# Moving the rank-one products, the query decay and the pooling sums of a retention-and-experts step between engines

## The reference, cut to what matters

```python
def step(S, xs):                      # prompt: two chunks of 128 rows, 4 heads
    qc, kc, vc = xs
    scores = jnp.einsum('bhid,bhjd->bhij', qc, kc) * mask
    intra = jnp.einsum('bhij,bhjv->bhiv', scores, vc)
    cross = jnp.einsum('bhid,bhdv->bhiv', qc * q_dec[..., None], S)
    S_new = S * c_dec[:, None, None] + jnp.einsum('bhjd,bhjv->bhdv', kc * k_dec[..., None], vc)
    return S_new, intra + cross
```

```python
outs.append((hi - lo) / cnt[None, :, None])
pooled = jnp.concatenate(outs, axis=-1) - p.astype(jnp.float32)
```

## Time and profile before

| what | us |
|---|---|
| median of 3 runs | 1198.78 |
| the three runs | 1196.62, 1198.78, 1198.88 |
| the profiled execution's own time | 1199.12 |
| its span, first to last instruction | 1197.3 |
| the mixer, routing included, about | 0 to 280 |
| experts, about | 280 to 1197 |

### The profile page before, as it was taken

One profiled execution on the slowest core, in us unless ns is written; L12 is line 12 of the kernel. 1 busy time (PEld: TensorE's weight loads), 2 busy tenths in 40 slices (PEclk: granted clock), 3 DMA queues, 4 the chain that ended last, 5 costly groups with the idle time before them and its releaser, 6 DMA issues.

```text
span 1197.3 us, 15344 instructions
## 1 busy us (share of the span) xinstructions
PE 1141.8 (95%) x5979; PEld 587.2 (49%) x5979; DVE 387.9 (32%) x881; ACT 188.1 (16%) x432; POOL 40.9 (3%) x69
## 2 busy tenths in 40 slices
PE   9989989999999999999989999989998989999997
PEld 7988979985433334333434333434333333333342
DVE  5667755762222122222212121213121212121222
ACT  2132423012011101111010101010101101010112
POOL 3106000000000000000000000000000000000000
PEclk9999989999999999999999999999999999999999
DMA  9753668897999999999999999999999999999996
GB/s 321 226 200 107 226 206 316 291 347 302 426 416 428 426 431 426 429 430 431 423 434 426 434 427 434 423 431 427 436 425 435 421 430 429 436 424 430 427 420 251
DMA packets 66810, 455.22 MB, mean 380 GB/s; under 512 B 4321, under 2 KB 39597, under 8 KB 45760
## 3 DMA queue, kind: packets, MB, share of 16 engines
q1 hardware_dynamic: 64544, 447.99, 90.9%
q0 software_dynamic: 1872, 5.95, 1.5%
q10 hardware_dynamic: 344, 0.61, 0.1%
HBM read 448.65 MB, written 6.11 MB: 380 GB/s over the span
## 4 chain that ended last, share of the span: by engine, by line
PE 62%; DMA 32%; DVE 2%; ACT 1%; SPq 1%; issue 1%; DVEq 0%; ACTq 0%
PE psum L1376 23%; DMA ring<-in_w_down 20%; PE psum L1387 11%; PE psum L1121 11%; DMA ring<-in_w_gate_up 11%; PE psum L1463 4%; PE psum L1286 3%; PE psum L1443 1%; PE psum L1497 1%; PE psum L1148 1%; PE psum L1453 1%; SPq L700 1%; PE psum L1498 1%; DMA ring<-in_w_in 1%; DMA ring<-v_rows 1%
## 5 line engine op out<-in xcount | busy, mean ns | idle before, releaser
L1376 PE MATMUL psum<-ring,x_T 128*64 128x512 f32 x1004 | 454.3, 598 | 9.6 <-DMA ring<-in_w_gate_up 8.9
L1377 PE MATMUL psum<-ring,x_T 128*64 128x512 f32 x994 | 449.3, 599 | 0.0
L1376 PEld LDWEIGHTS psum<-ring,x_T 128*64 128x64 f32 x1004 | 130.5, 137 | 274.2 <-issue 251.8
L1387 PE MATMUL psum<-ring,act_T 128*64 128x512 f32 x960 | 219.1, 610 | 23.2 <-DMA ring<-in_w_down 23.2
L1387 PEld LDWEIGHTS psum<-ring,act_T 128*64 128x64 f32 x960 | 71.1, 140 | 159.3 <-issue 141.7
L1377 PEld LDWEIGHTS psum<-ring,x_T 128*64 128x64 f32 x994 | 129.1, 137 | 0.0
L2517 DVE TENSOR_TENSOR h_raw<-psum,params 128x512 f32<-128x512 f32 x32 | 22.1, 691 | 299.7 <-PE psum L1443 299.7
L2534 DVE TENSOR_TENSOR z_T<-z_T,psum 128x264 f32<-128x264 f32 x112 | 43.0, 426 | 204.5 <-PE psum L1498 204.5
L1121 PE MATMUL psum<-x_sums,ring 128*128 128x132 f32 (+1 forms) x512 | 68.1, 283 | 7.0 <-ACT qk L1727 5.0
L1463 PE MATMUL psum<-normed,one_hot 128*128 128x512 f32 x168 | 74.4, 592 | 0.0
L1121 PEld LDWEIGHTS psum<-x_sums,ring 128*128 128x128 f32 x512 | 63.8, 195 | 7.9 <-ACT qk L1727 5.4
(11 more groups left out here) (347 smaller groups left out, 1002.9 us busy)
## 6 DMA issues: line engine op xcount, KB each, us to landing
ring<-in_w_gate_up SPq DMA_DIRECT2D x32, 4096.0 KB, 31.7
ring<-in_w_gate_up SPq DMA_DIRECT2D x59, 2048.0 KB, 29.7
ring<-in_w_down SPq DMA_DIRECT2D x56, 2048.0 KB, 33.5
ring<-in_w_in SPq DMA_DIRECT2D x21, 1024.0 KB, 6.3
ring<-in_w_down SPq DMA_DIRECT2D x12, 1024.0 KB, 27.3
spare<-in_w_gate_up SPq DMA_DIRECT2D x5, 1280.0 KB, 36.7
ring<-in_state_ret POOLq DMA_DIRECT2D x8, 512.0 KB, 7.7
ring<-v_rows SPq DMA_DIRECT2D x8, 512.0 KB, 8.9
```

What stands on the lines that cost most here:

```text
L1376: mm(psum[0:CAP, 2 * j + n], x, gate, start=first, stop=final)
L1377: last = mm(psum[CAP:P, 2 * j + n], x, up, start=first, stop=final)
L1387: last = mm(psum[j * CAP:(j + 1) * CAP, 4 + n], hidden[:, j, 4 * h + i], w, start=h == 0 and i == 0, stop=h == 1 and i == 3)
```

## The change

Four things move, and no arithmetic is left out.

1. GpSimd issues the loads of states 4 to 7 once the last value tile is done (`tile_done`), ahead of the store of the value rows; before, they stood behind it. The spread of rows 0 to 3 moves from behind the chunk of group 4 to behind the chunk of group 5 (`SPREAD_AT` 8 to 9).
2. Rank-one products 0 to 3 stay on ScalarE but move into groups 4 and 5 (one each) and group 6 (two). Products 4 to 7 go to GpSimd, as one 128x1024 operation each.
3. The decayed queries are made by GpSimd, two operations of 128x512; TensorE's products o and one `more_sums` of VectorE wait for them by `pool_step`.
4. GpSimd's pooling sums begin only when VectorE has written the norm of o (1).

```diff
-RANK_ONE_AT = {1: (0,), 2: (1,), 3: (2,), 4: (3, 4), 5: (5,), 6: (6, 7)}
-SPREAD_AT = 8
+SPREAD_AT = 9
...
+            pool.wait_ge(u_ready, KD)
+            pool.wait_ge(tile_done, done_count(V0 + 7))
+            for b in range(4, NS):
+                pool.dma_start(state_s(b), state_ret[0, b].rearrange("h d v -> d h v")).then_inc(state_in[b], 16)
             pool.wait_ge(aux_took, AUX_AT[("v", 7)] + 1)
             for h in range(H):
                 pool.dma_start(v_rows[:, h], v_few[32 * h:32 * h + NS]).then_inc(v_saved, 16)
-            pool.wait_ge(u_ready, KD)
-            for b in range(4, NS):
-                pool.dma_start(state_s(b), state_ret[0, b].rearrange("h d v -> d h v")).then_inc(state_in[b], 16)
+
+            def rank_one(b):
+
+                pool.wait_ge(spread_in[b % 4], 16 * (b // 4 + 1))
+                nc.gpsimd.tensor_tensor(spread_v[:, b % 4], spread_v[:, b % 4],
+                                        k_cols[:, :, b:b + 1].broadcast_to([P, H, DV]),
+                                        ALU.mult).then_inc(rank_one_ready, 1)
...
             step(nc.gpsimd.tensor_copy(k_cols, k_T[:, :, NPR:NT]))
+            pool.wait_ge(roped, 8)
+            pool.wait_ge(product_done, PRODUCT_AT[3, 3])
+            for c in range(2):
+                step(nc.gpsimd.tensor_tensor(qd[:, c], q_T[:, :, c * P:(c + 1) * P],
+                                             const("q_dec").rearrange("p (h i) -> p h i", h=H), ALU.mult))
 
             n = NM + NPR
+            pool.wait_ge(aux_took, AUX_AT[("o", 1)] + 1)
             for g, w in enumerate(WINDOWS):
...
             nc.gpsimd.memset(both_squares, 0.0).then_inc(zeroed, 1)
+            pool.wait_ge(rank_one_ready, 4)
+            for b in range(4, NS):
+                rank_one(b)
...
+                    pe.wait_ge(pool_step, 2 + c)
...
+                    if g >= GATE_FROM - 2:
+                        rank_one(g - GATE_FROM + 2)
...
+                    if g == GATE_FROM:
+                        rank_one(2)
...
                     if g == GATE_FROM:
+                        rank_one(3)
                         root(0)
...
-                    for b in RANK_ONE_AT.get(g - GATE_FROM, ()):
-                        rank_one(b)
...
-                    V.tensor_tensor(qd[:, c], q_T[:, :, c * P:(c + 1) * P],
-                                    const("q_dec").rearrange("p (h i) -> p h i", h=H), ALU.mult)
...
                 elif g == GATE_FROM + 1:
                     dve.wait_ge(aux_took, AUX_AT[("score", 1)] + 1)
+                    dve.wait_ge(pool_step, 3)
```

## The result

The changed kernel takes 1185.51 us (median of 4 runs, 1184.83 to 1186.14) and the kernel before, in the same runs, 1198.83 (1196.62 to 1200.83). The ratio is 0.9889, interval 0.9871 to 0.9907: faster by 13.3 us. The profiled execution of after took 1186.14 us, its span is 1184.3 (before 1199.12 and 1197.3), the mean granted clock 0.992 (before 0.988).

What follows compares the result with a forecast made beforehand. It took TensorE's mixer stops for ScalarE's copies, with the half clock behind them, as the cost to remove: 1199.1 less 10.0 (stops), less 4.5 (clock), plus 0.9 (chunk of group 6), plus 1.7 (competition) gives 1187.2 us, range 1183 to 1190.

Steps and rivals of the forecast that it cites:

- The stops, 10.0: TensorE's waits in the mixer for ScalarE's copies (5.0, 3.0 and 2.0 us) all go, saving 10.0 us.
- the clock, 4.5: Half-speed clock after TensorE's two long mixer stops goes with them, saving 1.65 + 2.9 = 4.5 us.
- Part 1: Earlier state loads: group 4's chunk lands at 60.0, not 63.8; 3.0 us stop goes; queue sharing delays group 3's 2.3 us.
- The chunk of group 6, +0.9: Spread rows ahead of group 6's chunk delay it; TensorE waits longer at the meta state, +0.9 us (0 to 2).
- Part 2: Rank-one products: ScalarE's fit idle time, GpSimd's take 2.6 us each; 5.0 + 2.0 us of TensorE stops go.
- Part 3 and 4: Query decay on GpSimd is worth nothing; later pooling sums move their competition with VectorE into groups 7 to 10.
- Competition, +1.7: GpSimd's work lengthens VectorE's operations in groups 7 to 13, costing 1.7 us, bounds 0 and 9.6.
- rival D: Gain hidden by the experts' weight stream if not tied to the mixer: 1193 to 1199 us, chance 0.06.
- A: First TensorE stop stays because early states delay group 3's chunk: 1191.8 us, chance 0.11.
- B: GpSimd's lock holds VectorE, the 9.6 us reach TensorE nearly whole in groups 9 to 12: 1193 us, chance 0.13.
- E: Slower: GpSimd holds the lock through pooling and products, stalling VectorE in groups 7 to 14: 1208.4 us, chance 0.04.
- C: GpSimd's last product takes ScalarE's place, the 4.7 us stop and its clock stay: 1194.8 us, chance 0.04.

Runs made afterwards that it cites:

- experiment 2: Changed kernel with the state loads behind the value-row saves again and the spread rows behind group 4's chunk again: 1188.17 us, ratio 0.9907.
- experiment 3: Changed kernel with rank-one products 4 to 7 back on ScalarE in their old places: 1193.73 us, ratio 0.9959.
- experiment 6: Changed kernel with only the state loads late again, spread rows still behind group 5's chunk: 1188.34 us, ratio 0.9921.
- experiment 12: Second run of the changed kernel with spread rows 0 and 1 behind group 5's chunk, 2 and 3 behind group 6's: 1183.72 us, ratio 0.9888.
- experiment 1: Kernel before with only the early state loads and the spread rows behind group 5's chunk: 1196.86 us against 1199.0, ratio 0.9978.
- experiment 7: Changed kernel with the pooling sums started as soon as their input is there: 1187.9 us, ratio 0.9905.
- experiment 8: Changed kernel with the query decay back on VectorE: 1185.57 us, ratio 0.9898.
- experiment 9: Changed kernel with three more GpSimd operations reading two SBUF inputs behind each of products 4 to 7: 1199.16 us, ratio 1.0005.
- experiment 10: Changed kernel with seven GpSimd memory fills behind each of products 4 to 7: 1185.4 us, ratio 0.9899.
- experiment 11: Changed kernel run again unaltered, beside the one with divided spread rows: 1186.30 us, ratio 0.9902.
- Experiment 4: Changed kernel with spread rows 0 and 1 behind group 5's chunk and 2 and 3 behind group 6's: 1183.35 us, ratio 0.9868.

## Why the prediction was right, step by step

**The stops, 10.0, and the clock, 4.5.** Both went, and are worth 15.6 together instead of 14.5. The difference is that TensorE's shift at each stop is 0.2 to 0.3 larger than its idle time in the profile; why is not shown. Experiments 2, 3 and 6 bring the two long stops back one at a time with their causes.

**Part 1.** The landing of group 4's chunk (59.55, 60.0 predicted) and the 3.8 us were right. The sharing of the queues was not, at least in after's execution: group 3's chunk landed 5.2 us after its issue and not 7.3 (the 2.3 us was 2.1 by its own terms, 4.3 less 2.2). In the other executions with early states it took 5.2 to 5.3, but 6.6 in experiment 3 and 6.4 in experiment 12, and no stop followed. The states took their 8.6 us beside it, the first one landing at 50.83, 2.8 us behind the chunk. The Trainium skill, "DMA: Bandwidth & Descriptors", section "Queues, rings and completion order", has each engine take turns between its queues; the 2.3 us worked out from that supposed that both have data to move from the start, and most landings here do not bear it out. Nothing else hung on it, as 2.6 us of idle (54.44) stood behind.

**The chunk of group 6, +0.9.** The direction was right and the size low: 1.4 at the wait, within the 0 to 2. What I missed is its second price. In seven of eight profiled executions with 2.2 to 3.1 us at the meta state (experiments 1, 3 and 7 to 11; the eighth is the one of after) the clock fell to 0.50 behind it, for 3.4 us in six and 6.8 in experiment 1. I had charged the clock to the stops that go and not to the one that grows. That after's profiled execution escaped it is luck: the forecast's clock of 1.00 throughout the mixer holds there and not in the same kernel's other trace (experiment 11), where it costs 1.7 us. Experiment 4 shows that it need not be paid at all.

**Part 2.** ScalarE's early products (1.70 each, the first at 74.99) cost nothing, and it has no wait for `v_rows` in the mixer. The GpSimd products took 1.90 to 2.36 us where I took 2.6, the last one done at 154.86, and `next_state` for it starts at 155.7 without a wait. Experiment 3 prices this part at 8.2 us. Experiment 1 against 3 shows that the stop of 1.7 us and a small one go with the early place of products 0 to 3, or with parts 3 and 4, which both also moved there; experiments 7 and 8 undo these last two one by one, and neither stop comes back.

**Part 3 and 4.** Nothing, as put (experiment 8); for the pooling sums by the trace alone.

**Competition, +1.7.** It was nothing. VectorE's operations were lengthened as predicted, to 1.15 at 132.45 beside GpSimd's operation behind the pooling sums and to 2.27 beside a product, but the slack in each group held all of it. (The idle time to be left in groups 7 to 13 was 10.4 us and not 10.1, since the stop of 0.31 us lies ahead of that window.) The forecast took a value close to its lower end and the truth was that end; experiment 9 shows how much more would have been needed.

**The sum.** The terms of stops and clock 1.1 too small, meta state 0.5 too small, start 0.6 not in it, competition 1.7 too large: the mixer ends 14.8 us earlier, where 11.9 was predicted. The span gains 13.0, since the part behind the mixer lasted 926.9 instead of 925.0. I do not read a cause into these 1.9, although experts longer than before was one of the signs of being wrong: over the other kernels' profiled executions that part lasts 924.8 to 926.1 whenever the mixer ends, between 255.8 and 273.2 us. About 0.9 of the 1.9 stands ahead of TensorE's last matmul and the rest behind it. So the tie of the weights to the mixer (rival D) gave nothing back that can be told from scatter. That the forecast of 1187.2 lies so near the measured 1185.51 owes something to luck as well: the mixer did 2.9 us better than the sum and the part behind it 1.9 worse.

**Rivals.** A: no stop from the states in any trace with early states. B and E: the mechanism is real, but it does not reach TensorE at four products (experiment 9). C: VectorE does not wait for the last product. D: nothing of it seen.

## What to carry to other kernels

A stop of TensorE costs its idle time and the half clock that comes with it; when a change shifts a wait instead of removing it, charge the clock to the wait that grows as well. Moving products to GpSimd was free here as long as each group had slack for one held VectorE operation per GpSimd operation that reads SBUF; count those, not their busy share. A block of loads put between two others delays the one behind it, so divide it by the idle behind each before choosing a single place for it.

## What the runs showed of the hardware

- Four 512 KB loads issued by GpSimd right behind a 1 MB load of SyncE barely touched it in most executions (5.2 to 5.3 us from issue to landing, 5.0 alone), but it took 6.6 us in experiment 3 and 6.4 in experiment 12. The first of the four landed 6.3 to 7.6 us after its issue.
- A stop of 2.2 to 3.1 us of TensorE is followed by half clock in most executions but not in all of the same program (2.26: none; 2.58: 3.4 us), and its length differs (3.4 us in most, 6.8 in two). The experts of before show the same: behind eight stops of 2.5 to 2.8 us the clock fell five times. None followed the stops of up to 1.7 us in the mixer. In the stops of 4.7 to 5.4 us the clock falls before the stop ends. Over all the mixers here, the half clock lasted 6.8 us each of the six times that it began before the stop was over, and 3.4 each of the nine times that it began behind it.
- The product of 128x1024 with one input spread over the columns takes GpSimd 1.90 us where no VectorE operation with two SBUF inputs was under way as it began (133.70), less than four times the 0.73 of the earlier trace rows.
- VectorE and GpSimd take turns when both have a queue of operations that read two inputs from SBUF: 1.84 us per VectorE operation, beside GpSimd operations of 1.5 to 1.9 us (experiment 9).
- Start-up took 4.0 us longer in one of the fourteen profiled executions (experiment 7) and differed by up to 1.1 us among the others; TensorE's first matmuls took nearly twice as long in it (1.97 us against 1.09 for the same eight).
